# Sample rows stacked by feature halves, with their memory output and transposes moved on TensorE, in a hybrid GDN/MLA/MoE streaming step

## The chip, the cores and the metric

One Trainium2 chip, one core of it. The metric is device time of one launch in microseconds (us), lower is better. Three runs of the kernel before gave 1286.77, 1288.47 and 1288.25 us, median 1288.25. TensorE is called PE here, VectorE DVE, ScalarE ACT, GpSimd POOL and SyncE SP; SP issues nearly all DMAs.

## The reference

A one-layer step over 256 prompt rows and 64 sample rows of width 1024. Three residual blocks follow one another; the last two matter here:

```python
h = rms_norm(x, p['norm_mem'])
... # 4 heads over 256 memory tokens: om
x = x + om.reshape(B, S, MEM_HEADS * MEM_HEAD_DIM) @ p['w_mo']

h = rms_norm(x, p['norm_ffn'])
logits = (h @ w_router + b_router).astype(F32)
top_val, top_idx = lax.top_k(logits, TOP_K)          # 4 of 32 experts
gate = jax.nn.softmax(top_val, axis=-1)
...
gu = xb @ w_gu[e] + b_gu[e]                          # 1024 -> 2048
act = gt * jax.nn.sigmoid(SWIGLU_ALPHA * gt) * (up + 1.0)
return act @ w_down[e] + b_down[e]                   # 1024 -> 1024
```

All is float32. Every one of the 32 experts has 8 MB of gate and up weights and 4 MB of down weights, and all are read once.

## The kernel before, in words

**Rows.** The 320 rows are three blocks of up to 128: b = 0 and 1 are the prompt, b = 2 the 64 sample rows, which use 64 of the 128 partitions. `x3` holds the residual rows [128, block, 1024], `xs3` the normalized ones, `xparts` their split into three bf16 parts whose sum is the float32 value, `hT` the rows transposed for the router.

**Before the experts.** `attention("mem", ...)` runs ten units of memory attention. Between its units PE first writes the rows of x back from the feature-major `xT` (`x_and_mem_out`, six blocks of four transposes, one half row block each, ACT copies each out with `x2_rows`), then multiplies heads by `w_mo` (`mem_out(b, half)` for the prompt blocks), and DVE adds the product to `x3` (`x3_add`). Behind the last unit the order on PE is written out by hand: `router(0)`, `rows_feature_major(1)`, `mem_out_pair()` (the sample block's product, its two column halves into banks 4 and 5), `router(1)`, `rows_feature_major(2)`, `router(2)`. A router is eight matmuls of 32 columns over the feature chunks. After each `x3_add` of a block, ACT sums its squares (`square_rows`), POOL takes the root, DVE scales (`x3_scale`), and ACT and DVE make the three bf16 parts (`part`, `x3_rest`, `last_part`). DVE picks the top four of each block (`top_k`), PE ranks the rows within an expert (`ranks`, `counts`, bank 3), DVE turns the ranks into a 0/1 matrix per expert (`slots`), and PE gathers 64 rows for expert 0 with it (`first_gather`, 72 bf16 matmuls).

**The expert loop.** Expert e has six weight tiles of 2 MB (four of `w_gu`, two of `w_down`). Nine tiles fit on the chip (`SLOTN = 9`). SP loads tiles 0 to 8 as their places come free before the loop and then tile n as soon as PE has used tile n - 9:

```python
sp.wait_ge(sem("x3_mm"), 2 * TB)        # w_mo is no longer read
first_tiles(1, 2)
first_tiles(TILES, TILES + 1)
sp.wait_ge(sem("lg_mm"), TB)            # all three routers done
first_tiles(TILES + 1, SLOTN - 1)
...
sp.wait_ge(sem("tile_used"), i * (TURN * TILES) + (n - SLOTN + 1))
```

In iteration e PE does `gate_up` (with the `scatter` of expert e - 1 between its tiles), `gather(e + 1)` and `down(e)`; ACT does the sigmoid and copies, DVE the SwiGLU, `slots`, and `accumulate`: six multiply-adds of 512 columns into `x3`, two per block. After the last expert the rows are scattered and accumulated and SP stores six pieces (L578).

Of the kernel before, what the change touches and what calls it, by code (L numbers as in the profile page):

```python
# [15 lines left out]
BF16 = mybir.dt.bfloat16  # L16
# [72 lines left out]
def trunk_kernel(nc, x_prompt, x_sample, cache_kv_latent, cache_k_rope, state_gdn, state_conv, cache_mem_k,  # L89
# [5 lines left out]
    with ctx:  # L95
# [5 lines left out]
        def sem(name):  # L101
# [7 lines left out]
            "tensor": ["gains_tr", "rbc02_mm", "rbc1_mm", "conv_tr", "ab_tr", "gcum_mm", "gbc_mm", "qm_mm", "rank_mm", "cnt_mm", "start_mm",  # L109
# [186 lines left out]
        xparts = V[:, 0:4608].bitcast(BF16).rearrange("p (b s d) -> p b s d", b=TB, s=3)  # L296
# [12 lines left out]
        rpos = KT[:, 256:355].rearrange("p (b e) -> p b e", b=TB)  # L309
        mask = KT[:, 356:452].rearrange("p (b e) -> p b e", b=TB)  # L310
# [120 lines left out]
        def _(sp):  # L431
# [114 lines left out]
            sp.wait_ge(sem("x3_mm"), 2 * TB)  # L546
# [21 lines left out]
            def store_rows(b):  # L568
                rows = P if b < 2 else DEC
                dst = yp[0][b * P:b * P + rows, :] if b < 2 else ys[0]  # L570
                sp.dma_start(dst, x3[0:rows, b, :]).then_inc(sem("st_out"), 16)

            for n in range(2 * TB):
                b, c = n // 2, 512 * (n % 2)
                rows = P if b < 2 else DEC
                dst = yp[0][b * P:b * P + rows, :] if b < 2 else ys[0]
                sp.wait_ge(sem("acc_done"), (E - 1) * (2 * TB) + n + 2)
                sp.dma_start(dst[:, c:c + 512], x3[0:rows, b, c:c + 512]).then_inc(sem("st_out"), 16)  # L578
            with sp.If(n_extra > 0):
# [6 lines left out]
                for b in range(TB):  # L586
                    store_rows(b)
                sp.wait_ge(sem("st_out"), 16 * (3 * TB))
# [5 lines left out]
        def _(pool):  # L594
# [23 lines left out]
            for b in range(TB):  # L618
                if b == 1:
# [4 lines left out]
                    pool.memset(mask, 0.0)  # L624
                    pool.memset(gate, 0.0)
# [11 lines left out]
        def _(act):  # L637
# [380 lines left out]
            def square_rows(b):  # L1018
                act.wait_ge(sem("x3_add"), 2 * b + 2)
                act.activation(xs3[:, b, :], x3[:, b, :], ACT.Square, accum_out=ssq[:, 8 + b:9 + b]).then_inc(sem("x3_sq"), 1)  # L1020

            def rows_feature_major(b):
                rows = P if b < 2 else DEC
                for half in range(2):
                    act.wait_ge(sem("blk_tr"), 2 * TB + 2 * b + half + 1)
# [3 lines left out]
            def part(b, i):  # L1029

                act.wait_ge(sem("xs_ready"), 2 * b + i + 1)
                run(xparts[:, b, i, :], xs3[:, b, :]).then_inc(sem("x3_part"), 1)

            def x2_rows(i):
                b, half = i // 2, i % 2
                rows = P if b < 2 else DEC
# [3 lines left out]
                run(x3[0:rows, b, 512 * half:512 * half + 512], PS[6 + half][0:rows, :]).then_inc(sem("x2_ev"), 1)  # L1040

            def first_block(n):
                if X2_AT <= n < X2_AT + 2 * TB:
                    x2_rows(n - X2_AT)
# [10 lines left out]
            part(1, 1)  # L1055
            square_rows(2)
            rows_feature_major(2)
            part(2, 0)
            part(2, 1)
            act.wait_ge(*at("top_ready"))  # L1060
            for b in range(TB):
                rows = P if b < 2 else DEC
                run(gate[0:rows, b, :], lg[0:rows, b, 0:E], ACT.Exp, bias=ntop[0:rows, b:b + 1]).then_inc(sem("gate_exp"), 1)
# [26 lines left out]
        def _(pe):  # L1090
# [532 lines left out]
            def mem_out(b, half):  # L1623
# [3 lines left out]
                if b == 0:  # L1627
                    pe.wait_ge(sem("x2_ev"), 5 + half)
# [9 lines left out]
            def mem_out_pair():  # L1638

                pe.wait_ge(sem("att_o"), ATT["mem"] + UNITS)  # L1640
                for h in range(H):
                    for side in range(2):
                        m = mm(PS[4 + side][half(side), :], om[:, h, 2 * P:2 * P + DEC], wmo_sb[:, h, 512 * side:512 * side + 512],
                               h == 0, h == H - 1)
                m.then_inc(sem("x3_mm"), 2)

            def rows_feature_major(b):
                rows = P if b < 2 else DEC
                for half in range(2):
                    pe.wait_ge(sem("x3_add"), 2 * b + 1 + half)  # L1650
                    for k in range(4):
                        m = tr(PS[6 + half][:, k * P:k * P + rows], x3[0:rows, b, (4 * half + k) * P:(4 * half + k + 1) * P])
                    m.then_inc(sem("blk_tr"), 1)

# [935 lines left out]
```

## Time and profile before

| | us |
|---|---|
| median of three runs | 1288.25 |
| the profiled execution | 1286.78 |
| its span, first to last instruction | 1285.0 |
| PE busy | 1254.3 |
| DVE busy | 459.5 |
| ACT busy | 207.8 |
| mean granted PE clock | 0.995 of full speed |
| DMA moved | 439.06 MB, mean 342 GB/s |

The profiled execution took 1.78 us more than its span. Engine rows are records of one execution; a PE that is busy may still be waiting inside its pipeline, so a busy share of 98% says little by itself. PE's rows come as weight loads (PEld) and matmuls (PE); one float32 matmul of the program is two of each, a transpose one of each. The granted clock is given as a share of 2.4 GHz: 1.00 is 2.4 GHz, 0.50 is 1.2 GHz.

### The profile page before, as it was taken

The page shows a single profiled execution, that of the slowest core. Times are in us where ns is not written, and L with a number is a line of the kernel's source. Part 1 is how long each engine was busy: PE and PEld are TensorE (multiplying, and loading weights), DVE is VectorE, ACT ScalarE, POOL GpSimd, SP SyncE. Part 2 cuts the span into 40 slices and gives each one's busy share as a digit, 9 for nine tenths or more (in the row PEclk, how much of TensorE's full clock was granted, in tenths as well). Part 3 has the DMA queues.
Part 4 walks back from the last instruction along what each step waited for, and adds up shares of the span by engine and source line. Part 5 has one row for each costly group of instructions (what it writes and reads, how often), then busy time and mean ns, then how long its engine had stood idle before and what let it go on. Part 6 is the DMA issues. An engine that isn't in the chain of part 4 may idle for free.

```text
span 1285.0 us, 20897 instructions
## 1 busy us (share of the span) xinstructions
PE 1254.3 (98%) x8556; PEld 574.0 (45%) x8556; DVE 459.5 (36%) x970; ACT 207.8 (16%) x547; POOL 18.2 (1%) x34
## 2 busy tenths in 40 slices
PE   8999999999999999999999999999999999999997
PEld 5677654576653333333333333343333334333332
DVE  4454334525572223333322332332232333222233
ACT  2542433623420000000000000000000000000000
POOL 0000001100000000000000000000000000000000
PEclk9999999999989999999999999999999999999999
DMA  9611011953089999999999999999999999999996
GB/s 311 254 66 67 2 30 26 322 251 145 4 358 429 427 426 430 427 429 427 429 427 429 427 429 428 429 428 429 428 429 427 429 427 429 427 429 427 430 427 266
DMA packets 48768, 439.06 MB, mean 342 GB/s; under 512 B 8677, under 2 KB 11213, under 8 KB 24058
## 3 DMA queue, kind: packets, MB, share of 16 engines
q1 hardware_dynamic: 48492, 438.32, 81.9%
q8 instruction: 28, 0.46, 0.1%
q10 hardware_dynamic: 238, 0.20, 0.1%
q14 instruction: 10, 0.08, 0.0%
HBM read 435.17 MB, written 3.33 MB: 341 GB/s over the span
## 4 chain that ended last, share of the span: by engine, by line
PE 80%; DMA 16%; ACT 1%; DVE 1%; issue 1%; SPq 0%; DVEq 0%; POOLq 0%; POOL 0%; ACTq 0%
PE bank L1092 78%; DMA weights<-in_w_gu 16%; PE bank L1095 2%; ACT scaled L639 1%; DMA x<-in_x_sample 1%; PE bank L1755 0%; DVE x L2509 0%; ACT weights L639 0%; ACT small_weights L639 0%; DVE scaled L1970 0%; ACT scaled L1020 0%; DVE x L2180 0%; DVE stats L2284 0%; DVE small_weights L2361 0%; DVEq L2545 0%
## 5 line engine op out<-in xcount | busy, mean ns | idle before, releaser
L2509 DVE SCALAR_TENSOR_TENSOR x<-bank,small_weights,x 128x512 f32<-128x512 f32 (+1 forms) x192 | 134.9, 744 | 598.5 <-PE bank L1092 598.5
L1092 PE MATMUL bank<-weights,small_weights 128*64 128x512 f32 x1360 | 308.7, 596 | 3.6 <-DMA weights<-in_w_gu 3.1
L1092 PEld LDWEIGHTS bank<-weights,small_weights 128*64 128x64 f32 x1360 | 92.4, 136 | 188.8 <-issue 170.2
L1092 PE MATMUL bank<-weights,scaled 128*64 128x512 f32 x704 | 155.9, 595 | 5.1 <-ACT scaled L639 5.1
L1092 PE MATMUL bank<-small_weights,weights 128*128 128x320 f32 (+4 forms) x400 | 110.0, 422 | 0.1
L1092 PE MATMUL bank<-scaled,small_weights 64*128 64x512 f32 x384 | 108.1, 640 | 1.4 <-DVE x L2509 0.7
L639 ACT ACTIVATE scaled<-scaled 128x512 f32<-128x512 f32 x32 | 20.1, 630 | 548.8 <-DVE scaled L1901 548.8
L639 ACT ACTIVATE scaled<-bank 128x512 f32<-128x512 f32 (+6 forms) x145 | 54.8, 406 | 325.8 <-PE bank L1092 244.7
L1092 PEld LDWEIGHTS bank<-weights,scaled 128*64 128x64 f32 x704 | 48.7, 137 | 97.1 <-issue 87.7
L1092 PE MATMUL bank<-stream,small_weights 128*64 128x512 f32 (+4 forms) x408 | 87.4, 544 | 1.5 <-DMA stream<-in_w_gu 1.1
L1092 PEld LDWEIGHTS bank<-stream 128*128 128x128 bf16 (+1 forms) x2416 | 75.0, 100 | 27.6 <-issue 26.4
L1092 PE MATMUL bank<-small_weights 96*64 96x512 bf16 (+2 forms) x408 | 87.1, 499 | 0.0
L1092 PEld LDWEIGHTS bank<-small_weights,weights 128*128 128x128 f32 (+2 forms) x400 | 72.0, 191 | 27.9 <-issue 1.4
L1092 PE MATMUL bank<-stream 128*128 128x64 bf16 (+1 forms) x2416 | 79.2, 196 | 0.3 <-DVE stream L1897 0.3
L1092 PEld LDWEIGHTS bank<-scaled,small_weights 64*128 64x128 f32 x384 | 29.0, 184 | 79.0 <-issue 75.9
L1092 PE MATMUL bank<-weights 64*64 64x64 f32 (+5 forms) x752 | 62.4, 266 | 0.0
L1092 PEld LDWEIGHTS bank<-small_weights 96*64 96x64 bf16 (+2 forms) x408 | 28.8, 128 | 69.2 <-issue 67.9
L1092 PE MATMUL bank<-small_weights,stream 128*128 128x320 f32 (+4 forms) x212 | 54.4, 410 | 0.5 <-DVE small_weights L2298 0.5
L1092 PEld LDWEIGHTS bank<-stream,small_weights 128*64 128x64 f32 (+1 forms) x408 | 30.6, 143 | 50.8 <-issue 44.6
L1092 PEld LDWEIGHTS bank<-weights 64*64 64x64 f32 (+3 forms) x752 | 38.1, 144 | 22.1 <-issue 21.1
L1092 PEld LDWEIGHTS bank<-small_weights,stream 128*128 128x128 f32 (+1 forms) x212 | 35.2, 187 | 14.8 <-issue 1.9
L1092 PE MATMUL bank<-more_weights,small_weights 128*64 128x512 f32 x176 | 40.2, 599 | 0.5 <-DMA more_weights<-in_w_gu 0.5
(207 smaller groups left out, 879.8 us busy)
## 6 DMA issues: line engine op xcount, KB each, us to landing
weights<-in_w_gu SPq DMA_DIRECT2D x85, 2048.0 KB, 26.9
weights<-in_w_down SPq DMA_DIRECT2D x44, 2048.0 KB, 28.3
stream<-in_w_gu SPq DMA_DIRECT2D x21, 2048.0 KB, 28.1
more_weights<-in_w_gu SPq DMA_DIRECT2D x11, 2048.0 KB, 27.6
small_weights<-in_w_gu SPq DMA_DIRECT2D x11, 2048.0 KB, 26.2
small_weights<-in_w_down SPq DMA_DIRECT2D x10, 2048.0 KB, 28.2
more_weights<-in_w_down SPq DMA_DIRECT2D x10, 2048.0 KB, 28.4
weights<-in_w_in SPq DMA_DIRECT2D x3, 2048.0 KB, 14.0
```

The source lines that it names most:

```text
L639: return act.activation(out, in_, func, **kw)
L1092: return pe.matmul(out, lhsT, rhs, start=start, stop=stop)
L1095: return pe.transpose(out, in_, ident[0:in_.shape[0], 0:in_.shape[0]])
L2509: dve.scalar_tensor_tensor(xx, PS[bank][0:rows, :], gcur[0:rows, b:b + 1], xx, ALU.mult, ALU.add)\
```

## The change

The 64 sample rows become a [128, 512] tile: partitions 0 to 63 hold features 0 to 511 of them, partitions 64 to 127 features 512 to 1023 (`x3s`, `xs3s`, `sparts`). What ran over 64 partitions and 1024 columns now runs over 128 partitions and 512 columns, and what ran twice for the sample block's halves runs once, where that is possible. The row sum of squares is then in two parts, which a small matmul with `eye2` adds (`sample_sum`), and ACT takes the root as Ln and Exp instead of POOL. The router of the sample rows is computed twice, once for each half of the partitions, so that the mask and gates stand on both. The PE order behind the attention becomes `rows_feature_major(1)`, `mem_out_pair()`, `router(0)`, `rows_feature_major(2)`, `router(1)`, `sample_sum()`, `router(2)`. In the core of the diff a line of "..." marks what is left out:

```diff
-            router(0)
             rows_feature_major(1)
             mem_out_pair()
+            router(0)
+            rows_feature_major(2)
             router(1)
-            rows_feature_major(2)
+            sample_sum()
             router(2)
...
-            sp.wait_ge(sem("x3_mm"), 2 * TB)
+            sp.wait_ge(sem("x3_mm"), HALVES)
...
             def mem_out_pair():
-                        m = mm(PS[4 + side][half(side), :], om[:, h, 2 * P:2 * P + DEC], wmo_sb[:, h, 512 * side:512 * side + 512],
+                        m = mm(PS[4][half(side), :], om[:, h, 2 * P:2 * P + DEC], wmo_sb[:, h, 512 * side:512 * side + 512],
...
+            def sample_sum():
+                pe.wait_ge(sem("x3_sq"), TB)
+                for side in range(2):
+                    m = mm(PS[5][half(side), 0:1], eye2, ssq[:, 10:11])
+                m.then_inc(mark("pair_mm"), 1)
...
             def router(b):
-                    m = mm(PS[b][0:rows, 0:E], hT[:, k, b * P:b * P + rows], wr_sb[:, k, :], k == 0, k == KD - 1)
+                    if b < 2:
+                        m = mm(PS[b][:, 0:E], hT[:, k, b * P:(b + 1) * P], wr_sb[:, k, :], k == 0, k == KD - 1)
+                    else:
+                        for side in range(2):
+                            m = mm(PS[2][half(side), 0:E], hT[:, k, 2 * P:T], wr_sb[:, k, :], k == 0, k == KD - 1)
...
-            for b, a in ((0, 0), (1, 0), (1, 1), (2, 0), (2, 1)):
-                ranks(b, a)
+            ranks(0, ones, 1, n=3, begin=True)
+            ranks(1, ones, 2, n=2)
+            ranks(0, ustrict, 0)
+            ranks(1, ustrict, 1)
...
             def x_and_mem_out(n):
-                    for k in range(4):
-                        m = tr(PS[6 + half][0:rows, k * P:(k + 1) * P], xT[:, 4 * half + k, b * P:b * P + rows])
+                    if b < 2:
+                        for k in range(4):
+                            m = tr(PS[6 + side][:, k * P:(k + 1) * P], xT[:, 4 * side + k, b * P:(b + 1) * P])
+                    else:
+                        for k in range(4):
+                            for s in range(2):
+                                m = mm(PS[6][half(s), k * P:(k + 1) * P], xT[:, 4 * s + k, 2 * P:T], ident)
...
             def gather_pass(terms, begin, end):
+                        if b == 2:
+                            m = mm(xg_pair[:, :, k, :], sparts[:, i, k * P:(k + 1) * P], S[:, 2, :, :], False, last)
+                            continue
...
             def scatter(it, b, bank=6, added=None):
+                if b == 2:
+                    mm(PS[bank][:, :], slotT[:, 2 * P:3 * P], y_sb).then_inc(sem("scat_mm"), 1)
+                    return
...
             # ACT, behind the attention
             part(1, 0)
-            part(1, 1)
             square_rows(2)
             rows_feature_major(2)
+            sample_rstd()
+            part(1, 1)
             part(2, 0)
...
             # DVE, behind the attention
-            top_k(0)
             x3_scale(1)
+            x3_add(4)
+            top_k(0)
             x3_rest(1)
-            x3_add(4)
-            x3_add(5)
             top_k(1)
...
             def accumulate(it, e, second=6):
-                for n in range(2 * TB):
+                for n in range(HALVES):
```

`HALVES` is 2 * TB - 1 = 5. `slots` becomes two operations (256 and 128 columns), the mask of the sample block two of 64 partitions, and the three gate divisions one. The number, size and order of the DMAs are the same.

On PE, behind the last attention unit, before the change. The 128x32 and 64x32 rows are the routers, 128x128 and 128x64 of L1095 the transposes of rows, 64x512 the sample block's memory output, `const` the ones and triangle of the ranks (a row counts the program's matmuls):

```order
L1092 MATMUL bank<-stream,small_weights 128x32 x8
L1095 MATMUL bank<-const,x 128x128 x8
L1092 MATMUL bank<-weights,stream 64x512 x8
L1092 MATMUL bank<-stream,small_weights 128x32 x8
L1095 MATMUL bank<-const,x 128x64 x8
L1092 MATMUL bank<-stream,small_weights 64x32 x8
L1092 MATMUL bank<-stream,const 128x32 x5
L1092 MATMUL bank<-const,stream 32x1 x2
L1092 MATMUL bank<-stream,const 128x32
```

The same place after the change:

```order
L1107 MATMUL bank<-const,x 128x128 x8
L1104 MATMUL bank<-weights,stream 64x512 x8
L1104 MATMUL bank<-stream,small_weights 128x32 x8
L1668 MATMUL bank<-const,x 128x64 x8
L1104 MATMUL bank<-stream,small_weights 128x32 x8
L1104 MATMUL bank<-stats,const 64x1 x2
L1104 MATMUL bank<-stream,small_weights 64x32 x16
L1104 MATMUL bank<-stream,const 128x96
L1104 MATMUL bank<-stream,const 128x64
L1104 MATMUL bank<-stream,const 128x32 x2
L1104 MATMUL bank<-const,stream 32x1 x2
L1104 MATMUL bank<-stream,const 128x64
```

The memory output stands ahead of both prompt routers, the sample's transposes between them, and the last router has sixteen matmuls in place of eight.

On DVE, the same stretch after the change (L1937 is `x3_scale`, L1933 128x512 `x3_add(4)`, L2452 to L1933 128x32 one `top_k`, L1933 128x1024 `x3_rest(1)`):

```order
L1937 TENSOR_SCALAR scaled<-x,stats 128x1024
L1933 TENSOR_TENSOR x<-x,bank 128x512
L2452 SCALAR_TENSOR_TENSOR stream<-bank,stats,gain_rows 128x32
L2453 MAX stream<-stream 128x8
L2454 COPY stream<-stream 128x4
L1937 TENSOR_SCALAR stream<-stream 128x1
L2457 MATCH_REPLACE stream<-stream 128x36
L1933 TENSOR_TENSOR stream<-stream 128x32
L1933 TENSOR_TENSOR scaled<-scaled,stream 128x1024
```

Before, `top_k(0)` stood ahead of `x3_scale(1)`, and two additions of 64x512 behind `x3_rest(1)`.

## Rows read from the trace of the kernel before

**Rows 1.** The page, rate of the DMAs in 40 slices of 32.1 us

```profile
GB/s 311 254 66 67 2 30 26 322 251 145 4 358 429 427 426 430 427 429 427 429 427 429 427 429 428 429 428 429 428 429 427 429 427 429 427 429 427 430 427 266
```

**Rows 2.** Chain that ended last, in order of time: start us, us, what

```profile
470.88 27.28 PE bank L1092 x186
...
499.09 27.28 PE bank L1092 x186
...
1046.32 38.99 DMA weights<-in_w_gu
```

**Rows 3.** Timeline of SP's DMA issues: start us, us, line, transfer

```profile
355.05 0.33 SPq L433 DMA_DIRECT2D weights<-in_w_gu  x1
...
359.11 0.33 SPq L433 DMA_DIRECT2D small_weights<-in_w_gu  x1
371.51 0.35 SPq L556 DMA_DIRECT2D weights<-in_w_gu  x1
375.22 3.75 SPq L556 DMA_DIRECT2D weights<-in_w_down  x2
```

**Rows 4.** Windows: stretch, length, busy PE PEld DVE ACT POOL, PEclk, DMA share, GB/s

```profile
370.00:372.00 2.00, 2.00 (x12) 0.60 (x10) 0.69 (x5) 0.00 (x0) 0.00 (x0) 1.00 0.71 303
372.00:374.00 2.00, 2.00 (x14) 0.60 (x12) 0.71 (x4) 0.00 (x0) 0.00 (x0) 1.00 0.77 172
```

**Rows 5.** Timeline behind the attention: start us, us, engine, line, operation, count

```profile
348.65 1.87 PE L1092 MATMUL bank<-stream,small_weights 128*128 128x32 f32 x16
...
349.05 0.68 DVE L1897 TENSOR_TENSOR x<-x,bank 128x512 f32<-128x512 f32 x1
...
351.36 3.65 PE L1092 MATMUL bank<-weights,stream 128*64 128x512 f32 x16
...
351.84 0.14 PEld L1092 LDWEIGHTS bank<-weights,stream 128*64 128x64 f32 x2 [0.29 <-issue]
...
354.94 1.86 PEld L1092 LDWEIGHTS bank<-stream,small_weights 128*128 128x128 f32 x16 [0.81 <-issue]
...
355.06 1.40 DVE L1897 TENSOR_TENSOR x<-x,bank 64x512 f32<-64x512 f32 x2
...
356.84 0.57 PEld L1095 LDWEIGHTS bank<-const,x 64*128 64x128 f32 x8
...
357.96 1.01 PEld L1092 LDWEIGHTS bank<-stream,small_weights 128*64 128x64 f32 x16 [0.55 <-ACT small_weights L639]
...
359.01 1.19 PEld L1092 LDWEIGHTS bank<-stream,const 128*128 128x128 f32 x10
...
359.26 0.24 DVE L2414 SCALAR_TENSOR_TENSOR stream<-bank,stats,gain_rows 64x32 f32<-64x32 f32 x1
...
360.53 1.22 DVE L1897 TENSOR_TENSOR scaled<-scaled,stream 128x1024 f32<-128x1024 f32 x1
...
360.65 0.50 PEld L1092 LDWEIGHTS bank<-stream,const 128*128 128x128 f32 x2 [0.21 <-DVE stream L2438]
...
362.21 0.56 DVE L1897 TENSOR_TENSOR stream<-const,stream 128x384 bf16<-128x384 f32 x1
...
362.83 4.02 PE L1092 MATMUL bank<-stream 128*128 128x64 bf16 x72 [0.34 <-DVE stream L1897]
```

**Rows 6.** Windows of PE alone: stretch, length, busy, PEclk, DMA share, GB/s

```profile
360.50:360.75 0.25, 0.12 (x2) 0.69 1.22 524
...
367.25:367.50 0.25, 0.00 (x0) 0.66 1.32 524
```

**Rows 7.** Timeline: an x block's transposes, and the end of the program

```profile
322.84 0.44 PEld L1095 LDWEIGHTS bank<-const,scaled 128*64 128x64 f32 x4
...
1265.12 2.16 PEld L1092 LDWEIGHTS bank<-stream 128*128 128x128 bf16 x72 [0.81 <-issue]
...
1277.35 4.03 DVE L2509 SCALAR_TENSOR_TENSOR x<-bank,small_weights,x 128x512 f32<-128x512 f32 x6 [9.14 <-PE bank L1092]
1278.13 4.60 SPq L578 DMA_DIRECT2D out<-x  x6
```

More of the change, by code:

```diff
@@ L617, in _ @@
                 taken += 1
-            for b in range(TB):
+            for b in range(2):
                 if b == 1:
@@ L1039, in x2_rows @@
                 act.wait_ge(sem("blk_tr"), i + 1)
-                run(x3[0:rows, b, 512 * half:512 * half + 512], PS[6 + half][0:rows, :]).then_inc(sem("x2_ev"), 1)
+                run(x3[:, b, 512 * half:512 * half + 512] if b < 2 else x3s, PS[6 + half][:, :]).then_inc(sem("x2_ev"), 1)
             def first_block(n):
-                if X2_AT <= n < X2_AT + 2 * TB:
+                if X2_AT <= n < X2_AT + HALVES:
                     x2_rows(n - X2_AT)
@@ L1061, in _ @@
             for b in range(TB):
-                rows = P if b < 2 else DEC
-                run(gate[0:rows, b, :], lg[0:rows, b, 0:E], ACT.Exp, bias=ntop[0:rows, b:b + 1]).then_inc(sem("gate_exp"), 1)
+                run(gate[:, b, :], lg[:, b, 0:E], ACT.Exp, bias=ntop[:, b:b + 1]).then_inc(sem("gate_exp"), 1)
             def sigmoid(it):
@@ L1627, in mem_out @@
                 if b == 0:
-                    pe.wait_ge(sem("x2_ev"), 5 + half)
+                    pe.wait_ge(sem("x2_ev"), HALVES)
                 else:
@@ L1690, in _, with ranks @@
             pe.wait_ge(*at("wr_ready"))
-            router(0)
             rows_feature_major(1)
             mem_out_pair()
+            router(0)
+            rows_feature_major(2)
             router(1)
-            rows_feature_major(2)
+            sample_sum()
             router(2)
-            def ranks(b, a):
-                return mm(PS[3][:, b * E:(b + 1) * E], ustrict if a == b else ones, mask[:, a, :], a == 0, a == b)
+            def ranks(b, lhsT, first, n=1, begin=False, end=False):
+                return mm(PS[3][:, first * E:(first + n) * E].rearrange("p (b e) -> p b e", b=n), lhsT,
+                          bcast(mask[:, b, :], [P, n, E], 1) if n > 1 else mask[:, b:b + 1, :], begin, end)
             def counts(b):
@@ L1834, in down, with scatter @@
                     m.then_inc(sem("tile_used"), 1)
-            def scatter(it, b, bank=6, free=None):
+            def scatter(it, b, bank=6, added=None):
                 if b == 0:
@@ L1840, in scatter @@
                     pe.wait_ge(sem("slotT_ready"), it + 1)
-                pe.wait_ge(sem("acc_done"), it * (2 * TB) + (2 * (b if free is None else free) + 1))
-                for half in range(2):
-                    part = slice(64 * half, 64 * half + 64)
-                    mm(PS[bank + half][:, :], slotT[part, b * P:(b + 1) * P], y_sb[part, :])\
-                        .then_inc(sem("scat_mm"), 1)
+                pe.wait_ge(sem("acc_done"), it * HALVES + (((0, 2, 3)[b] if added is None else added) + 1))
+                if b == 2:
+                    mm(PS[bank][:, :], slotT[:, 2 * P:3 * P], y_sb).then_inc(sem("scat_mm"), 1)
+                    return
+                for side in range(2):
+                    mm(PS[bank + side][:, :], slotT[half(side), b * P:(b + 1) * P], y_sb[half(side), :]).then_inc(sem("scat_mm"), 1)
             pe.wait_ge(*at("top_ready"))
```

179 lines of the change are left out of this document (97 added, 82 removed).

## The prediction

> **What bounds the kernel now.** I read the page's slices first, then the chain, then SP's queue, and only then the stretch that the change touches. The slices show the DMAs at 426 to 430 GB/s from the thirteenth (385 us) to the last but one [rows 1]; nothing in the kernel moves data faster for long. The chain seems to say something else: PE holds it with one expert every 28.21 us (499.09 - 470.88) up to about 1046 us, and only then do DMA waits of some 39 us appear [rows 2]. Both are true. One expert is 12.58 MB, which at 428 GB/s takes 29.4 us; PE is 1.2 us faster per expert, eats the lead that nine resident tiles give it, and waits for weights in the end. So the time is **the moment from which the DMAs run without a pause, plus the bytes behind it, plus a tail**. In SP's queue [rows 3] that moment is the issue of tile 9 at 371.51, released by PE's first used tile of expert 0. Ahead of it, tiles 1 and 6 go out at 355.05 (`w_mo` free) and tile 7 at 359.11 (routers done); they are done shortly before tile 9 starts, and in 370 to 374 us the DMAs are idle for about 0.58 + 0.46 = 1.04 us [rows 4]. Behind that they never stop. A microsecond by which expert 0 starts later is a microsecond at the end; PE time saved inside the loop is worth nothing.
>
> **Work saved in the loop: 0.** Per expert the gather has 60 weight loads in place of 72 (72 take 2.16 us [rows 7], 30 ns each; a matmul of 128 columns replaces two of 64), the scatter one matmul less, DVE one multiply-add less (4.03/6 = 0.67 us [rows 7]); against them `slots` is two operations. That is some 0.3 to 0.5 us of PE per expert, 10 to 15 us in all, and it is covered by the weight stream. If that cover were gone it would be the whole gain.
>
> **Ahead of expert 0, at full clock.** The order on PE decides. Before: router(0) from 348.65, the pair from 351.36, router(1) from 354.94, transposes from 356.84, router(2) from 357.96 to about 359.0 [rows 5].
> - The transposes of block 1 now come where router(0) stood. Their second half needs the addition of 349.05 to 349.73 [rows 5], which router(0) used to hide. PE waits some 0.6 us, then four transposes (half of eight, about 0.5 us): the pair starts at 350.3, 1.0 us earlier, and ends at 350.3 + 3.58 (354.94 - 351.36) = 353.9.
> - Behind it stand router(0) 1.9 (354.94 to 356.84), the sample's transposes 0.6 (0.57), router(1) 1.9, `sample_sum` 0.25 (two small matmuls at 0.12 each, as ten loads take 1.19) and router(2). That one has twice the matmuls: sixteen loads of 64 columns take 1.01 us [rows 5], so 2.1. Sum: 353.9 + 1.9 + 0.6 + 1.9 + 0.25 + 2.1 = 360.65, against 359.0: **+1.65**.
> - The addition for the sample rows is one operation instead of two (0.68 for 1.40), the square sum half as wide, and Ln and Exp replace POOL. All of that is done before router(2), so it is worth 0. If router(2) were not the last to arrive, the earlier addition would give up to 1.7 us.
> - `top_k(2)` took 359.26 to 360.53, 1.27 us; a second mask operation adds no more than the 0.24 of its first one [rows 5]. **+0.2**.
> - `x3_rest(2)`, 1.22 us from 360.53, held DVE while the last rank was done at about 361.2; at half the width it no longer does: **-0.45**. `slots` in two: **+0.1** (0.56 before).
> - So the gather would start at 362.83 + 1.5.
>
> **The clock.** PE's granted clock fell to 1.2 GHz at 360.6 and came back at 367.3 [rows 6]: 5.6 us after the last dense work (the pair, to 354.94), and 4.5 us into the dense gather. The gather ran at 53.6 ns per matmul, 3.86 us, where the same 72 take 2.16 to 2.3 at full clock [rows 7]. The record doesn't say how it would fall in another order, so I take the same distance: 353.9 + 5.6 = 359.5. Bounds: not before the gather (0), or right behind the pair (everything doubled, +6.7). From 359.5 the last 1.15 us of router(2) take twice as long: **+1.15**; that loads double is seen in the last rank, 2 loads in 0.50 against 10 in 1.19 [rows 5]. The ranks and counts of the prompt, hidden behind `top_k(2)` before, are then eight loads of 0.25 and four small ones, 2.4 us, against 1.7 of `top_k(2)`: **+0.7**. The gather at half clock is 48 x 0.0536 + 12 x 0.107 = 3.85: 0. For the clock's return I take the same distance into the gather: 0, between -1.6 (full clock throughout) and +1.8 (half of tile 0's 3.65 us more).
>
> **The rest.** The x blocks between the attention units are five instead of six. The fifth has eight matmuls of 64 columns' load, about twice the loads of a transpose (4 in 0.44 [rows 7]), so PE gains nothing, ACT one copy: **-0.2**, between -0.5 and +0.3. At the end DVE has five additions instead of six, but SP still stores six pieces, the last two at once; one issue, 0.33 us, then stands where 0.67 stood [rows 3, 7]: **-0.3**, between -0.6 and 0. Tiles 1 and 6 go out 1.0 us earlier and tile 7 about 3 us later, at a time when the DMAs still have 1 and 6 to move (10 us): 0.
>
> **Sum.** 1.65 + 0.2 - 0.45 + 0.1 + 1.15 + 0.7 - 0.2 - 0.3 = +2.85. On the profiled execution's 1286.78 that is 1289.6. That execution is one of the two low ones of four, 1.47 below the median; the others may have lost on the same clock what my sum already charges, so I add only 0.4 of it: **1290.0 us**, 0.14% above the median of 1288.25. A measurement of this kernel tells about 0.2%, 2.58 us, from no change: below 1285.67 is faster, above 1290.83 slower.
>
> **One rule against one row.** The forecast's largest term is the doubled router(2). Its two halves write different halves of the partitions. In the pair, where the halves also alternate, two loads of 64 columns take 0.14 us, and in router(2) sixteen take 1.01, 0.063 each [rows 5]: they stand one behind the other. The Trainium skill, TensorEngine Tiling (Array Packing), Key Properties, says that different tiles can execute weight loads and matmuls in parallel. By that rule the second set would be free; the trace disagrees as far as loads go. By rows the sum is the one above; what it would be otherwise is the first rival.
>
> **Rivals.**
> 1. *The halves of router(2) overlap.* It then takes 1.05, ends at 359.6, before the clock costs it anything: 2.85 - 1.05 - 1.15 = +0.65, 1287.4, or 1287.8 with the same 0.4. For it: matmuls of the pair, 0.46 us (3.65/8) per two of 512 columns, leave no room for the loads' whole length twice. Against it: the loads' spacing. Chance 0.14.
> 2. *The clock stays up, or is back early in the gather.* None of +1.15 and +0.7, and up to -1.6: -0.6, 1286.2, or 1286.6. For it: the routers are now packed without the 0.5 us pause before router(2). Against it: sparse work lasts from 353.9 to 364, longer than before. Chance 0.12.
> 3. *The clock falls earlier: slower than before.* Routers, sums and ranks are 32-column matmuls behind heavy loads, and there are more of them behind the pair. Falling at 356.4, before router(1), doubles 4.25 us instead of 1.15: +3.1, 1293.1. With a return only after tile 0, +1.8 more. It decides from a fall 0.8 us earlier than I took, since each microsecond costs one. Chance of a result above 1290.83 by it: 0.22.
> 4. *The loop counts after all.* If the weight stream sped up to PE's pace, 10 to 15 us would go: about 1276. Against it: the same 426 to 430 in every slice, whoever waits. Chance 0.02. That the change doesn't do what it says I see no way for: the order of both engines shows it.
>
> **The numbers.** The forecast's own case has 0.50; its range is 1288.4 to 1291.6, and of it 0.14 lies above 1290.83. Slower: 0.22 + 0.14 = 0.36. Faster: 0.02 of rival 4 and 0.03 of rival 2, 0.05. Within 0.2%: the remaining 0.59. Range 1286.8 to 1293.0: it takes in rival 1, about half of rival 2 and most of rival 3.
>
> **What would show it.** In the profile after: SP's issues at about 354 (two tiles), then tile 7 near 362 and tile 9 near 375 instead of 371.5, with a longer pause of the DMAs before it; router(2) as 32 loads in over 2 us; the clock at half before the router's end; the gather starting near 366.2; an iteration of about 27.8 us while PE is ahead, and waits for weights from earlier than 1046 us on; the same 427 GB/s. A tile 9 issued at 371.5 or earlier makes the forecast wrong, and so does a DMA rate that isn't the old one.

## The result, and the profile after

The changed kernel took **1290.24 us** (median of 20 runs) beside 1288.33 us of the kernel before (20 runs): a ratio of 1.0014, with a 95% interval of 1.0007 to 1.002. It is slower by 0.14%, under the 0.2% that count as a difference here. One of the 20 runs took 1323.78 us at a mean granted clock of 0.945 and is left out of the ratio. The profiled execution took 1288.87 us with a span of 1287.0, against 1286.78 and 1285.0 before.

SP's queue after, start us, us, line, transfer; it answers to [rows 3]:

```profile
354.56 0.33 SPq L437 DMA_DIRECT2D weights<-in_w_gu  x1
354.93 0.44 SPq L437 DMA_DIRECT2D stream<-in_w_gu  x1
361.68 0.33 SPq L437 DMA_DIRECT2D small_weights<-in_w_gu  x1
373.61 0.35 SPq L560 DMA_DIRECT2D weights<-in_w_gu  x1
```

Tiles 1 and 6 are asked for 0.5 us earlier than before, tile 7 2.6 us later and tile 9 2.10 us later. The windows of that stretch, columns as in [rows 4], show the pause of the DMAs grown from about 1 us to about 3:

```profile
370.00:372.00 2.00, 2.00 (x12) 0.65 (x10) 1.82 (x10) 0.00 (x0) 0.00 (x0) 1.00 0.48 197
372.00:374.00 2.00, 2.00 (x12) 0.64 (x10) 0.01 (x1) 0.00 (x0) 0.00 (x0) 1.00 0.02 8
```

From tile 9's issue to the end it is 1288.87 - 373.61 = 915.26 us, before 1286.78 - 371.51 = 915.27. So all that the change did to the time stands ahead of tile 9. PE's part of the timeline there, and two rows of DVE; it answers to [rows 5]:

```profile
349.14 0.60 PE L1107 MATMUL bank<-const,x 128*128 128x128 f32 x4
349.55 0.68 DVE L1933 TENSOR_TENSOR x<-x,bank 128x512 f32<-128x512 f32 x1
...
350.28 0.66 PE L1107 MATMUL bank<-const,x 128*128 128x128 f32 x4 [0.54 <-DVE x L1933]
350.87 3.65 PE L1104 MATMUL bank<-weights,stream 128*64 128x512 f32 x16
354.45 1.97 PE L1104 MATMUL bank<-stream,small_weights 128*128 128x32 f32 x16
...
356.75 2.81 PE L1104 MATMUL bank<-stream,small_weights 128*128 128x32 f32 x16
...
359.73 1.90 PE L1104 MATMUL bank<-stream,small_weights 128*64 128x32 f32 x32
361.56 1.92 PE L1104 MATMUL bank<-stream,const 128*128 128x96 f32 x8
...
363.32 0.69 DVE L1933 TENSOR_TENSOR scaled<-scaled,stream 128x512 f32<-128x512 f32 x1
...
365.71 3.23 PE L1104 MATMUL bank<-stream 128*128 128x64 bf16 x60
...
369.72 5.37 PE L1104 MATMUL bank<-weights,small_weights 128*64 128x512 f32 x24 [0.61 <-DVE small_weights L1933]
```

The pair (350.87) starts behind a bare wait of 0.54 us for DVE, which stands ahead of the second half of the transposes. In the trace of before, router(1) and router(2) are these rows:

```profile
354.94 1.97 PE L1092 MATMUL bank<-stream,small_weights 128*128 128x32 f32 x16
...
357.96 1.12 PE L1092 MATMUL bank<-stream,small_weights 128*64 128x32 f32 x16 [0.41 <-ACT small_weights L639]
```

So router(1) took 2.81 us in place of 1.97, and router(2), with 32 matmuls, 1.90 in place of 1.12. From the pair to the end of the gather no row of PE has a wait, yet its clock was at half, as windows of PE alone show (columns as in [rows 6]); the rows between these two are at 0.50, so it fell at 357.67 and came back at 367.91:

```profile
357.50:357.75 0.25, 0.25 (x4) 0.84 0.65 262
...
367.75:368.00 0.25, 0.25 (x7) 0.68 0.46 197
```

In the loop the chain of waits, which answers to [rows 2], gives an iteration of 782.82 - 754.64 = 28.18 us (before 28.21), and the DMAs' rate is the old one:

```profile
754.64 27.25 PE bank L1104 x172
782.82 27.25 PE bank L1104 x172
```

```profile
GB/s 312 252 66 68 1 30 33 323 241 146 2 339 428 427 428 427 430 428 428 429 427 429 428 429 429 427 429 427 430 429 427 429 427 430 429 427 430 427 429 265
```

### The profile page after: what moved, and what is told of

It is laid out like the page before. It is cut to its first block, busy times and chain, and to the rows that moved or that the text cites. A ratio compares the mean times of both kernels' runs of the same rounds, so it can differ in the third digit from the quotient of the medians.

```text
span 1287.0 us, 20024 instructions
## 1 busy us (share of the span) xinstructions
PE 1256.0 (98%) x8122; PEld 575.2 (45%) x8122; DVE 438.4 (34%) x966; ACT 206.3 (16%) x548; POOL 17.3 (1%) x31
## 4 chain that ended last, share of the span: by engine, by line
PE 80%; DMA 16%; ACT 1%; DVE 1%; issue 1%; ACTq 0%; DVEq 0%; SPq 0%
PE bank L1104 78%; DMA weights<-in_w_gu 16%; PE bank L1107 2%; ACT scaled L640 1%; DMA stream<-in_kv_a_norm 0%; PE bank L1794 0%; DVE x L2549 0%; ACTq L646 0%; DVE stats L2320 0%; ACT weights L640 0%; ACT small_weights L640 0%; DVE scaled L1933 0%; DVE x L2216 0%; DVEq L2585 0%; ACT stream L640 0%
## 5 line engine op out<-in xcount | busy, mean ns | idle before, releaser
L2549 DVE SCALAR_TENSOR_TENSOR x<-bank,small_weights,x 128x512 f32<-128x512 f32 x160 | 114.1, 747 | 599.4 <-PE bank L1104 599.4
L1104 PE MATMUL bank<-scaled,small_weights 64*128 64x512 f32 (+1 forms) x320 | 108.0, 641 | 0.7 <-ACT scaled L640 0.7
L1104 PEld LDWEIGHTS bank<-stream 128*128 128x128 bf16 (+1 forms) x2020 | 71.6, 99 | 27.4 <-issue 26.4
L1104 PE MATMUL bank<-stream 128*128 128x64 bf16 (+2 forms) x2020 | 77.4, 201 | 0.1
L1104 PEld LDWEIGHTS bank<-scaled,small_weights 64*128 64x128 f32 (+1 forms) x320 | 28.9, 185 | 78.4 <-issue 75.9
```

The lines of the kernel that those rows point to most:

```text
L1104: return pe.matmul(out, lhsT, rhs, start=start, stop=stop)
L2549: dve.scalar_tensor_tensor(xx, PS[bank][:, :], gcur[:, b:b + 1], xx, ALU.mult, ALU.add)\
```

## The experiments

Each run is read by two numbers: its ratio to the kernel before, and, from its profile, **D9**, the distance from the start of the prompt's last memory output (eight matmuls of 512 columns, 345.16 us before, 345.66 after) to tile 9's issue. D9 leaves out what varies earlier in the program. D1 is the same for tile 1, which the pair releases. "Rest" is the profiled time less tile 9's issue. The ratio is taken against runs of before from the same session (medians there 1288.08 to 1288.44), not against the table's first row. D1, D9, rest and clock come from one execution each. The same code from the last memory output to tile 9 gave a D9 of 27.95 in after and loop_more and of 29.1 in gather6 and split_x, while the ratios of after, gather6 and split_x are alike; a difference of D9 under about 1.2 us therefore shows nothing by itself where the clock fell.

| kernel | median us (runs) | ratio, 95% interval | D1 | D9 | rest | clock falls, us |
|---|---|---|---|---|---|---|
| before | 1288.33 (20) | | 9.89 | 26.35 | 915.27 | 360.6 |
| after | 1290.24 (20) | 1.0014, 1.0007 to 1.002 | 8.90 | 27.95 | 915.26 | 357.7 |
| router_twice | 1288.46 (10) | 0.9995, 0.9986 to 1.0004 | 9.88 | 26.34 | 915.93 | 362.1 |
| stack_alone | 1288.36 (11) | 1.0005, 0.9996 to 1.0014 | 9.89 | 26.11 | 915.22 | 361.9 |
| order_alone | 1290.07 (11) | 1.0015, 1.0006 to 1.0024 | 8.91 | 28.04 | 915.46 | 359.7 |
| warm | 1290.16 (11) | 1.0008, 0.9999 to 1.0017 | 8.91 | 27.62 | 915.53 | never |
| split_x | 1289.84 (11) | 1.0013, 1.0004 to 1.0022 | 8.91 | 29.11 | 915.42 | 359.8 |
| gather6 | 1290.13 (10) | 1.0015, 1.0005 to 1.0024 | 8.91 | 29.12 | 915.48 | 357.5 |
| late_first | 1291.37 (10) | 1.0022, 1.0013 to 1.0031 | 9.89 | 29.62 | 915.93 | 362.2 |
| loop_more | 1302.85 (4) | 1.0113, 1.0096 to 1.0129 | 8.90 | 27.95 | 929.15 | 358.1 |
| stack_warm | 1287.49 (11) | 0.9995, 0.9986 to 1.0004 | 9.88 | 24.63 | 917.44 | never |
| before_warm | 1288.31 (11) | 1.0001, 0.9992 to 1.001 | 9.89 | 25.39 | 916.48 | never |
| pair_first | 1288.68 (12) | 1.0001, 0.9992 to 1.0009 | 7.27 | 27.15 | 915.29 | 359.0 |
| pair_first_warm | 1292.79 (6) | 1.0034, 1.0022 to 1.0046 | 7.28 | 30.70 | 915.55 | 357.9 |

**The halves of the change.** order_alone is the kernel before with the new order on PE, ACT and DVE, the rows not stacked. This is the edit on PE's order:

```diff
-            router(0)
             rows_feature_major(1)
             mem_out_pair()
-            router(1)
+            router(0)
             rows_feature_major(2)
+            router(1)
             router(2)
```

> Kernel before, with only the order moved (block 1's transposes and the sample's memory output ahead of router(0), the sample's transposes ahead of router(1), DVE and ACT in the matching order). Theory A (the order costs: a bare wait of some 0.6 us, and more sparse work behind the last dense work, so that PE's clock falls before the routers are done): the pair starts 1.0 us earlier than before, the clock falls inside a router, tile 9 goes out 0.7 to 1.5 us later than 371.5, the time is 1 us above before. Theory B (the stacking costs, not the order): tile 9 within 0.3 us of 371.5, the same time as before.

stack_alone is the changed kernel with the old order (the same edit backwards, `sample_sum` behind `rows_feature_major(2)`).

> Kernel after, with only the order put back to that of before. Theory A: router(0) hides the addition again, the dense pair stands 1.0 us later, the clock falls later; tile 9 goes out at 372.0 to 372.8, the time is about 1 us below after. Theory B: tile 9 stays at 373.6 or so and the time at that of after.

The order alone costs what the whole change costs: 1.0015 against 1.0014, D9 28.04 against 27.95. The stacking alone can't be told from nothing, 1.0005 with an interval that holds 1. Tile 9's absolute time missed both windows (374.32 and 373.01), as these executions came to the last memory output 1.1 and 1.7 us later than that of before; by D9 it moved by +1.69 and -0.24 us. Its profile also prices router(2) at full clock:

```profile
359.51 1.13 PE L1104 MATMUL bank<-stream,small_weights 128*64 128x32 f32 x32 [0.24 <-ACT small_weights L640]
```

**Does the doubled router(2) cost anything?** router_twice is the kernel before with router(2) computed a second time into the upper half of its bank:

```diff
                     m = mm(PS[b][0:rows, 0:E], hT[:, k, b * P:b * P + rows], wr_sb[:, k, :], k == 0, k == KD - 1)
+                    if b == 2:
+                        m = mm(PS[b][rows:P, 0:E], hT[:, k, b * P:b * P + rows], wr_sb[:, k, :], k == 0, k == KD - 1)
```

> Kernel before, with router(2) also multiplied into the upper half of the partitions (nothing reads that). Theory of the prediction (weight loads of the two halves stand one behind the other): router(2) takes 2.1 us in place of 1.05 and tile 9 goes out 1 us later. Rival (the halves overlap entirely, as the kernel after at full clock and with the order of before showed, 32 in 1.13 us): router(2) takes 1.1 to 1.2 us and nothing else moves.

32 matmuls took 1.13 us, where the 16 of before took 1.12, and D9 is 26.34 for 26.35. The second set is free, with its weight loads.

**The clock.** warm is the changed kernel with 15 dense bf16 matmuls of 512 columns in three places, whose results nobody reads:

```diff
+            def fill(bank, n):
+                for _ in range(n):
+                    mm(PS[bank][0:64, :], sel, b3[:, 0:512])
...
             router(0)
...
+            fill(1, 5)
             rows_feature_major(2)
             router(1)
+            fill(2, 5)
             sample_sum()
...
+            fill(0, 5)
             pe.wait_ge(*at("mask_ready"))
```

> Kernel after, with fifteen extra dense bf16 matmuls of 512 columns (their products are overwritten): five behind router(0), five behind router(1), five while PE waits for the last mask. At full clock five take about 1.1 us, so PE gets some 2.2 us of work more ahead of router(2). Theory A (the order costs mainly through the clock, which is then at 1.2 GHz from a router to the gather): the clock stays at 2.4 GHz up to the gather, the gather takes about 2.2 us in place of 3.2 to 4.0, tile 9 goes out at 28.0 us or less behind the start of the prompt's last memory output (after 27.95, the same code in two other runs 29.1), in spite of the added work; the time is within 1 us of after or below it. Rival C (the clock is a bystander and the added order and waits cost): tile 9 2.2 us or more later than after and the time 2 us above it.

The clock never fell. Routers, last rank and gather ran at full speed:

```profile
367.59 2.37 PE L1104 MATMUL bank<-stream 128*128 128x64 bf16 x60 [0.60 <-DVE stream L1942]
```

Each five fillers took some 1.27 us of PE, 3.8 in all, and D9 was still no longer than after's (27.62). So in the new order the slow clock costs up to some 4 us, less what of the fillers lay in a pause of PE. The median is after's all the same (1290.16), as the fillers ate what the clock gave.

**The x blocks.** split_x spreads the sample block's eight matmuls over two gaps between attention units instead of one:

```diff
+                if n == X2_AT + 5:
+                    for k in range(4):
+                        m = mm(PS[6][half(1), k * P:(k + 1) * P], xT[:, 4 + k, 2 * P:T], ident)
...
-                            for s in range(2):
-                                m = mm(PS[6][half(s), k * P:(k + 1) * P], xT[:, 4 * s + k, 2 * P:T], ident)
+                            mm(PS[6][half(0), k * P:(k + 1) * P], xT[:, k, 2 * P:T], ident)
```

> Kernel after, with the sample's x block written back in two unit gaps (four matmuls each) instead of eight in one. Theory A (the 0.67 us that after loses between 316 and 327 us is the one long block of 1.03 us between two units): the first memory output of the prompt starts 0.3 to 0.7 us earlier than 327.15, and tile 9 by as much. Rival (the loss is the two-pass matmuls in place of one-pass transposes, wherever they stand): no more than 0.2 us comes back. The time can't tell: 0.5 us at most.

One half alone takes as long as both together do in after, whose row is this:

```profile
321.33 1.09 PE L1104 MATMUL bank<-const,scaled 128*64 128x128 f32 x16
```

and in split_x:

```profile
322.92 1.09 PE L1104 MATMUL bank<-const,scaled 128*64 128x128 f32 x8
...
325.23 1.09 PE L1104 MATMUL bank<-const,scaled 128*64 128x128 f32 x8
```

From the first block's transposes to the first memory output it is 12.40 us here, 11.52 after, 10.85 before and in order_alone. Neither side of the expectation came true: the split made it worse by 0.88 us, as the pair of halves overlaps here too. The median doesn't show the 0.88: 1289.84.

**The loop.** gather6 leaves the third bf16 part out of every gather in the loop, so its gathered rows are less exact:

```diff
-                gather_pass(ALL_PARTS, True, True).then_inc(sem("gather_mm"), 1)
+                gather_pass([(b, i) for b in range(TB) for i in range(2)], True, True).then_inc(sem("gather_mm"), 1)
```

> Kernel after, with the third bf16 part left out of every gather inside the loop (the rows of experts 1 to 31 are then rounded to two parts): 40 weight loads in place of 60, some 0.7 us less on PE per expert, 21 us in all. Theory A (the weight stream bounds the loop): the period of an expert is about 27.5 us while PE is ahead, the first wait for weights comes earlier than 1047 us, and the time stays within 0.5 us of after. Rival (PE bounds the first 23 experts and they count): up to 16 us faster.

The expected 27.5 us is a miss: the iteration stayed at 28.17 us. The first wait for weights did come earlier, at 1005.99 us, and the time stayed with after's.

```profile
952.56 25.09 PE bank L1104 x112
980.73 25.09 PE bank L1104 x112
```

The gather itself, with 40 matmuls, took 1.55 us in place of 2.24, 0.69 less. It lies beside the activation of expert e on DVE, and behind it PE now waits for DVE:

```profile
977.57 1.55 PE L1104 MATMUL bank<-stream 128*128 128x64 bf16 x40
...
979.75 0.75 PE L1107 MATMUL bank<-const,scaled 128*128 128x128 f32 x4 [0.46 <-DVE scaled L2539]
```

That is why PE's piece of the chain reads 25.09 for 27.25: the chain runs over DVE while the gather runs, and no more than 0.69 us of work is gone. A cheaper gather doesn't shorten even PE's own iteration, which I had taken as a gain that the weight stream covers. loop_more adds 24 matmuls to each gather:

```diff
+                gather_pass([(0, 0), (0, 1), (1, 0)], True, True)
                 gather_pass(ALL_PARTS, True, True).then_inc(sem("gather_mm"), 1)
```

> Kernel after, with 24 extra bf16 matmuls (a closed group that is overwritten) in every gather of the loop, some 0.75 us of PE per expert, 23 us in all. Theory A (the weight stream at 29.4 us per expert bounds the loop): the period while PE is ahead becomes about 28.9 us, the first wait for weights comes later than 1047 us, and the time stays within 0.5 us of after. Rival (PE's 28.2 us counts): about 17 to 23 us slower.

```profile
1226.89 27.95 PE bank L1104 x196
1255.77 27.95 PE bank L1104 x196
```

An iteration of 28.88 us, 0.70 more; the chain has no wait for weights left in it, and the time grew by 1303.13 - 1288.87 = 14.26 us (by the medians, 12.6). This is a miss for the theory, and less than the rival's 17 to 23; it shows how thin the cover is. Nine resident tiles, 44 us of transfer at 428 GB/s, put the DMAs ahead at the start, and most of PE's 31 x 1.2 = 37 us goes into eating that lead; it waits for weights from about 1046 us on [rows 2]. Of the 31 x 0.70 = 21.7 us added, 14.3 came through: only 7.4 us, 0.24 per expert, were free. **The 1.2 us per expert of the prediction don't cover what is added.** That they cover what is saved is argued from the DMAs' steady rate: no run made the iteration shorter.

**Slope one.** late_first adds 96 matmuls to expert 0's gather in the kernel before:

```diff
+                for _ in range(4):
+                    gather_pass([(0, 0), (0, 1), (0, 2)], True, True)
                 gather_pass([(0, 0), (0, 1), (0, 2), (1, 0), (1, 1)], True, False)
```

> Kernel before, with 96 extra bf16 matmuls ahead of the first gather (closed groups, their sums are overwritten). Theory A (time is the issue of tile 9 plus 915.3 us): tile 9 goes out 3 to 5 us later and the profiled time minus that moment stays between 915.2 and 915.5. Rival (the lead of nine resident tiles absorbs it): less than 1 us on the time.

Tile 9 went out at 376.06, 4.55 us later than before, and the profiled time was 5.21 longer. D9 grew by 3.27, the median by 2.9 (1288.44 for before in that session). The rest of 915.93 lies outside the expected 915.2 to 915.5. Over the eleven profiles other than loop_more with a D9 of 26 us or more, the rest is 915.2 to 915.9 us, while tile 9 ranges from 371.51 to 377.23.

**Is there a version below both?** If order and clock are the price, stacked rows in the old order with the clock held should win. stack_warm is stack_alone with six fillers, where PE waits anyway; before_warm is the kernel before with the same six (it has no `sample_sum`):

```diff
             rows_feature_major(2)
...
+            fill(2, 3)
             sample_sum()
             router(2)
...
+            fill(0, 3)
             pe.wait_ge(*at("mask_ready"))
```

> The stacked kernel in the order of before (stack_alone), with six dense bf16 matmuls of 512 columns added whose results nobody reads: three ahead of router(2), three ahead of the last rank, places where PE waits 0.24 and 0.46 us anyway. In stack_alone the clock fell at 361.85 us and the gather's 60 matmuls took 4.02 us. If the clock is worth what the prediction's terms say and six are enough to hold it, the last rank, the bias and the gather run at full clock (the gather in 2.4), some 1.9 + 0.3 us less, against some 0.7 us of fillers that the pauses do not cover: tile 9 some 1.5 us nearer to the prompt's last memory output than stack_alone's 26.11, a median near 1287, the first version below both kernels. Rival: six are too few, the clock falls at another place all the same, and the fillers only cost: +0.7, 1289. Second rival: the gather then waits for something that the slow clock hid (x3_part, slots), and the gain is lost: 1288.3.

> The kernel before with the same six fillers at the same two places, nothing else. Its gather took 4.02 us for 72 matmuls, half of them at half clock (the clock came back 4.5 us into it), its last rank 0.50. If the clock is the lever: gather in 2.4 to 2.6, tile 9 some 1 us nearer to the prompt's last memory output than 26.35, median near 1287.3. If six are too few: 1288.3 to 1289. Against stack_warm it tells whether the stacked rows help at all once the clock is up: the same within 0.3 us by my account of the loop, or up to 0.9 us for the stacked kernel if the missing wait for the wide x3_rest(2) counts.

The clock held, and D9 fell as expected, by 1.48 us against stack_alone and 0.96 against before. That the time followed can't be shown: 0.9995 and 1.0001, both intervals hold 1. The first reaches down to 0.9986, 1.8 us, so it doesn't exclude stack_warm's 1.72 us of D9 either. The medians are 1287.49, half a microsecond above what I expected, and 1288.31, a miss. On the profiled executions the time did not follow; stack_warm's, 1289.24 us, was the longest of its eleven runs. Its windows:

```profile
370.00:372.00 2.00, 2.00 (x12) 0.72 (x10) 0.14 (x2) 0.00 (x0) 0.00 (x0) 1.00 1.03 442
372.00:374.00 2.00, 2.00 (x12) 0.62 (x10) 0.46 (x3) 0.00 (x0) 0.00 (x0) 1.00 0.94 393
```

```profile
357.05 0.33 SPq L437 DMA_DIRECT2D weights<-in_w_gu  x1
...
371.80 0.35 SPq L560 DMA_DIRECT2D weights<-in_w_gu  x1
```

The DMAs have next to no pause any more, while in before they had one of 1.04 us [rows 4]. An earlier tile 9 can give no more than the pause ahead of it. The profiled time is then tile 1's issue plus 1289.24 - 357.05 = 932.2 us (before_warm 1288.31 - 356.33 = 932.0), and the rest behind tile 9 reads 917.4 and 916.5. **So I read the time as the later of two lines: tile 9's issue + 915.4, and tile 1's issue + 931 to 932.** The second is fitted to these profiles and known to about 1 us only. Less its pause, before stands 931.73 - 1.04 = 930.7 us behind tile 1 and after 934.31 - 3.0 = 931.3; stack_alone's profile ended 1288.23 - 356.79 = 931.44 behind it. The expectations below put the kernel before on both lines at once; by its own pause it stands about 1 us above the second. The 0.7 to 1.5 us by which stack_warm lies above these three stay unexplained.

By this reading a tile 9 that is more than that pause earlier needs an earlier pair too. pair_first is the changed kernel with the pair right behind the prompt's last memory output; the fill lines are in pair_first_warm alone:

```diff
-            rows_feature_major(1)
             mem_out_pair()
+            rows_feature_major(1)
             router(0)
...
+            fill(1, 3)
             rows_feature_major(2)
             router(1)
+            fill(2, 2)
...
+            fill(0, 3)
```

> The changed kernel with the sample rows' memory output (the pair) one place earlier, right behind the prompt's last memory output and ahead of block 1's transposes; nothing else. My theory by now has two lines for the time: tile 9's issue plus about 915.3 us, and the issue of tile 1 (released by the pair) plus about 932 us, since from there on the DMAs have work without a pause only if tile 9 is asked for in time. Stacked_warm stood on the second one (357.05 plus 932.2), the kernel before on both at once (355.05 plus 931.7, 371.51 plus 915.3). Here the pair starts at the last memory output plus 3.5 in place of 4.6 us and the bare wait of 0.54 us ahead of it is gone, so tile 1 goes out some 1.7 us earlier than in after (distance 7.2 in place of 8.90). But more sparse work stands behind the last dense block, and if the clock falls 3.2 us behind the pair, as in after, it falls in router(0) and doubles some 1.5 us more: distance of tile 9 from the prompt's last memory output 28 to 29, median 1290 to 1291. Rival: only the order of the waits counted, not the clock: distance 27.4, median 1289.7. A median below 1288 would make both wrong.

> pair_first with eight dense bf16 matmuls of 512 columns whose results nobody reads: three behind router(0), two behind router(1), three ahead of the last rank. If they hold the clock at full speed, the PE work up to tile 0 is that of stack_warm plus two fillers: tile 9 about 25 us behind the prompt's last memory output (stack_warm 24.63, before 26.35), tile 1 about 7.2 us behind it (before 9.89). Line of tile 9: 1.3 us below before; line of tile 1: 2.7 us below. So 1287.0, against stack_warm's 1287.5 (which stood on the line of tile 1), the first version with a chance of an interval below 1. Rival: the second line doesn't exist and stack_warm's profile was 2 us long for another reason: then the same as stack_warm plus 0.4, 1287.9. Rival 2: three us from the pair to the first filler are too many, the clock falls: 1289 or more.

pair_first has no bare wait and tile 1 out 1.63 us sooner after the memory output than after does. Its D9 is 0.80 shorter and its ratio 1.0001, so it takes back most of what the change lost (1288.68 for 1290.24) and no more. Both figures are below my expectation (28 to 29, 1290 to 1291) and nearer to the rival's (27.4, 1289.7), which counts the order of the waits alone; the clock fell all the same, 4.5 us behind the pair in place of the expected 3.2. How much of the gain is the wait and how much the clock isn't separated. pair_first_warm is a miss. The clock fell at 357.9 all the same, then the fillers ran at half speed too, and D9 grew to 30.70:

```profile
357.00:357.50 0.50, 0.50 (x7) 1.00 1.07 459
357.50:358.00 0.50, 0.50 (x6) 0.92 0.84 360
358.00:358.50 0.50, 0.50 (x4) 0.50 0.99 426
```

Three fillers behind router(0), where warm has five, did not hold it; from one arrangement to the next this can't be counted on. So no run tests the second line. No version was measurably below the kernel before.

## Why the prediction was right, and where its terms were not

The median came out 0.24 us above the forecast of 1290.0 and in the middle of its range. **The frame held**: the profiled time moved with tile 9's issue, one for one within 0.7 us, at an unchanged DMA rate, and the order on PE was what it cost. That the number came so near is luck: the terms were less good than their sum. As distances from the prompt's last memory output, after less before (the first three rows are running totals, the sum starts from the third):

| step | predicted | measured |
|---|---|---|
| the pair starts | -1.0 | 5.21 - 6.20 = -0.99 |
| router(2) ends | 1.65 + 1.15 = +2.8 | 15.90 - 13.85 = +2.05 |
| the gather starts | +3.35 | 20.05 - 17.67 = +2.38 |
| gather and transposes up to tile 0's first matmul | 0 | 4.01 - 4.80 = -0.79 |
| that first matmul to tile 9 | 0 | 3.89 - 3.88 = 0 |
| what comes before (the x blocks) | -0.2 | 345.66 - 345.16 = +0.50 |
| behind tile 9 | -0.3 | 0 |
| sum, profiled | +2.85 | +2.09 |

- *The doubled router(2), +1.05.* Wrong, it is 0 (router_twice, stack_alone). I read the spacing of its weight loads, 0.063 us each, as a limit. The Trainium skill, TensorEngine Tiling (Array Packing), Key Properties, says that different tiles can execute loads and matmuls in parallel; I let the row outweigh it, and the runs agree with the skill: 32 loads of 64 columns in the time of 16. The row was one of a single stream and said nothing of two.
- *The clock, +1.15 and +0.7.* The mechanism was right, its place not. I assumed 5.6 us behind the pair; it was 3.2. Router(1) took 0.85 us more (start to start 2.75 for 1.90), the sums 0.1 and router(2) 0.8, 1.7 in place of 1.15. Rival 3 had a fall at 356.4: the truth lay between it and the forecast. Had the second set of router(2) cost what I charged, at half clock 2.1, the result would have been about 1292.3, near rival 3's 1293.1.
- *The gather, 0.* The clock came back 2.2 us into it (367.91), not 4.5: 3.23 us for 4.02. This is nearly all of the -0.79. In stack_alone the same 60 took 4.02, in pair_first 3.62, so it varies.
- *The x blocks, -0.2.* Wrong in sign. I took the eight matmuls for no dearer than the two blocks of four transposes. From the first block to the first memory output it was 11.52 us for 10.85. Start to start the eight take 1.03 us where the two blocks take 0.43 and 0.44, so 0.16 of the 0.67; another 0.24 is a longer wait for DVE ahead of that memory output (0.62 for 0.38), and the rest wasn't traced. The copy that ACT saves didn't pay for it.
- *The loop, 0.* The price was right, the reason wrong. I charged 30 ns for each of the twelve loads saved, 0.3 to 0.5 us per expert, and held it for covered by the weight stream. There was nothing to cover: a gather of 60 matmuls, twelve of which move 128 columns in place of 64, takes as long as the 72 did, and the iteration is shorter by the same 0.03 us (28.18 for 28.21). Before, then after:

```profile
975.51 2.27 PE L1092 MATMUL bank<-stream 128*128 128x64 bf16 x72
```

```profile
976.90 2.24 PE L1104 MATMUL bank<-stream 128*128 128x64 bf16 x60
```

This is the error of router(2) once more, loads counted as time. The "27.8 us" that I named as a sign was a miss, and so was the first wait for weights from earlier than 1046 us on (1047.62). gather6 shows that even a real saving there would have met DVE. The scatter saved nothing either, as its one matmul of 128 rows takes the same 1.13 us as the two of 64 rows:

```profile
1262.30 1.13 PE L1104 MATMUL bank<-scaled,small_weights 128*128 128x512 f32 x2
```

- *The tail, -0.3.* DVE's additions took 3.39 for 4.03 us and SP's stores 3.98 for 4.60, but the span ended 2.86 us behind the last store's issue, before 2.27: from DVE's first addition to the end 7.62 us, before 7.65. Why the last store landed later isn't shown.

```profile
1279.38 3.39 DVE L2549 SCALAR_TENSOR_TENSOR x<-bank,small_weights,x 128x512 f32<-128x512 f32 x5 [9.14 <-PE bank L1104]
1280.16 3.98 SPq L576 DMA_DIRECT2D out<-x  x6
```

So the errors cancel: 1.05 for router(2), 0.79 for the gather, 0.3 for transposes and sums and 0.2 for the ranks were charged too much, 0.55 of clock, 0.7 of x blocks and 0.3 of tail too little. That leaves 0.8 too much on the profiled execution. A second pair of errors stands beside it: I had allowed that the medians move 1.1 us less than the profiled executions (+1.75 for +2.85), and they moved 0.2 less (1.91 for 2.09). Had I got router(2) alone right, I would have forecast rival 1's 1287.8, 2.4 us too low. What decides where the clock falls stays open. Measured from the start of the last memory output it fell 15.0 to 15.8 us on where router(0) stood ahead of the pair (before, router_twice, stack_alone, late_first) and 11.6 to 12.1 where the pair came first (after, gather6, split_x, loop_more, pair_first, pair_first_warm), but 13.5 in order_alone.

## What to carry to other kernels

Where a weight stream runs at the DMAs' full rate to the end, write the time as the latest of a few lines, each an issue plus the bytes behind it, and find out how far the next line lies below the first: here the next lay only about 1 us below, so that moving only the first could give little downwards and cost its full price upwards. Fewer matmuls are not yet less time: look for what they are to save in their own row first (72 in 2.27 us, 60 in 2.24), then in the iteration of the chain, where another engine may stand right behind (gather6). Moving a dense block ahead of sparse ones is not free even with the same instructions: it opened a wait that the sparse block had covered, and left more sparse work behind it to run at half the clock.

## What the runs showed of the hardware

- Matmuls that write different halves of the output partitions, in turn, overlap fully, loads included: 32 float32 matmuls of 32 columns in 1.13 us beside 16 in 1.12, and 16 of 128 columns in 1.09 beside 8 in 1.09.
- PE's clock can fall to 1.2 GHz while its rows show no wait (357.5 to 357.75 us, busy 0.25 of 0.25). With 15 or six fillers (warm, stack_warm, before_warm) it stayed at 2.4 GHz, with eight in another order (pair_first_warm) it fell 12.0 us behind the last memory output's start, as in after.
- The same code from the last memory output to tile 9 gave a D9 of 27.95 in after and loop_more and of 29.1 in gather6 and split_x. The clock fell 11.7 to 12.1 us behind the last memory output's start in all four, but came back 22.3 us behind it in after and loop_more (367.91, 368.36) and 25.5 and 25.3 in gather6 and split_x (371.19, 373.45). So PE stood at half clock for 10.2 us in the first two and for 13.7 in the others; in before it was 6.8.
- DVE sets the pace right behind PE in the loop: 0.69 us less of PE work in gather6 left the iteration at 28.17 us, with a wait of 0.46 for DVE, and 0.70 more in loop_more made it 28.88.
